# Two-tile recurrence units: where the contraction steps of the tiles stand among the seven levels

## The reference

```
def token_mixers(n, s0_fw, s0_bw, ...):
    p = n @ w_in
    v = to_heads(p[..., COL_V:COL_FFW])
    logf_fw, k_fw = hgrn2_forget(p[..., COL_FFW:COL_FBW], lb[0])
    logf_bw, k_bw = hgrn2_forget(p[..., COL_FBW:COL_Q], lb[1])
    q = to_heads(silu(p[..., COL_Q:COL_G]))
    o, s_fw, s_bw = hgrn2_bidir(q, v, logf_fw, k_fw, logf_bw, k_bw, s0_fw, s0_bw)
    ...
    u3 = short_conv(p[..., COL_HY:COL_MERGE], conv_w, conv_b)
    o_b = hyena(u3, kern, hy_bias)

def hgrn2_chunk_scan step:
    cum = cumsum(gb); decay = exp(cum[t] - cum[s]) for s <= t
    scores = einsum('bhtsd,bhsd->bhts', q[t] * decay, k)
    o = scores @ vb + (qb * exp(cum)) @ s
    s_new = exp(last) * s + einsum('bhsd,bhse->bhde', kb * exp(last - cum), vb)
```

## Time and profile before

| | |
|---|---|
| time, median of 3 runs | 3942.68 us (3938.78 to 3953.53) |
| time of the profiled execution | 3941.52 us |
| its span in the profile | 3939.7 us |
| mean granted clock of TensorE | 0.947 of full |
| PE busy | 3543.2 us, 90% of the span |
| DVE busy | 2002.5 us, 51% |
| ACT busy | 1182.0 us, 30% |
| POOL busy | 958.7 us, 24% |
| chain that ended last | PE 72%, DVE 17%, issue 6%, ACT 3% |

### The profile page before, as it was taken

How to read it: one execution, slowest core, us unless ns; L and a number is a source line. 1 busy time by engine, 2 the same in 40 slices (tenths; PEclk the granted TensorE clock), 3 DMA queues, 4 the chain that set the end, 5 groups by cost and what they waited for, 6 DMA issues and landing times.

```text
span 3939.7 us, 51314 instructions
## 1 busy us (share of the span) xinstructions
PE 3543.2 (90%) x18712; PEld 2882.8 (73%) x18712; DVE 2002.5 (51%) x3071; ACT 1182.0 (30%) x1638; POOL 958.7 (24%) x396
## 2 busy tenths in 40 slices
PE   6699999888788998999698888899999887898998
PEld 2278888777676767778577756788888666677887
DVE  5656441536654446883538666454341457662113
ACT  1132112334441123222333255321212343543222
POOL 1023222221121123444210100222223211113443
PEclk9799999998899999999899899899999988899999
DMA  4323331310122223553210010233331210112222
GB/s 179 101 96 128 124 126 70 128 59 27 33 86 67 62 91 128 182 181 125 100 40 26 33 43 22 73 119 128 117 112 64 72 43 28 54 34 79 96 96 91
DMA packets 101862, 341.43 MB, mean 87 GB/s; under 512 B 10159, under 2 KB 21551, under 8 KB 100240
## 3 DMA queue, kind: packets, MB, share of 16 engines
q1 hardware_dynamic: 82760, 301.90, 22.0%
q10 hardware_dynamic: 18952, 37.51, 2.7%
HBM read 325.21 MB, written 14.16 MB: 86 GB/s over the span
## 4 chain that ended last, share of the span: by engine, by line
PE 72%; DVE 17%; issue 6%; ACT 3%; DMA 1%; DVEq 0%; POOL 0%; ACTq 0%; POOLq 0%
PE ps L399 56%; PE ps L415 2%; PE ps L1478 2%; PE ps L1944 1%; PE ps L1489 1%; PE ps L871 1%; DVE u_Z L993 1%; DVE hid_lo L756 1%; DVE xx_lo L645 1%; DMA hyena_k<-fst 1%; DVE u_S L1031 1%; DVE u_P L1005 1%; PE ps L1930 1%; PE ps L1916 1%; PE ps L545 1%
## 5 line engine op out<-in xcount | busy, mean ns | idle before, releaser
L2203 POOL TENSOR_TENSOR wr_lo<-raw,wr_hi 128x1024 fp32r<-128x1024 f32 x392 | 958.5, 2446 | 2951.4 <-ACT wr_hi L455 2931.5
L399 PE MATMUL ps<-xx_hi,wr_hi 128*128 128x512 f32 x1840 | 742.2, 403 | 55.2 <-DVE xc_lo L649 44.0
L399 PE MATMUL ps<-xx_hi,wr_lo 128*128 128x512 f32 x1840 | 729.9, 397 | 0.0
L399 PE MATMUL ps<-xx_lo,wr_hi 128*128 128x512 f32 x1840 | 728.4, 396 | 0.0
L455 ACT ACTIVATE wr_hi<-raw 128x1024 fp32r<-128x1024 f32 x388 | 411.6, 1061 | 602.0 <-PE ps L399 569.3
L399 PEld LDWEIGHTS ps<-xx_hi,wr_hi 128*128 128x128 f32 x1840 | 349.7, 190 | 154.2 <-issue 36.2
L750 DVE TENSOR_TENSOR ff_raw<-ps,ff_gate 128x768 f32<-128x768 f32 (+1 forms) x88 | 72.6, 825 | 681.7 <-PE ps L399 678.7
L399 PEld LDWEIGHTS ps<-xx_lo,wr_hi 128*128 128x128 f32 x1840 | 350.1, 190 | 77.5 <-issue 2.2
L399 PEld LDWEIGHTS ps<-xx_hi,wr_lo 128*128 128x128 f32 x1840 | 349.6, 190 | 76.8
L500 DVE CUSTOM_DVE_ANT_0 ps<-raw,cb 128x1024 f32<-128x1024 f32 x240 | 379.9, 1583 | 50.5 <-DMA raw<-in_mod_stream 18.7
L399 PE MATMUL ps<-hid_hi,wr_hi 128*128 128x512 f32 (+1 forms) x1056 | 319.1, 356 | 9.3 <-DVE hid_lo L756 9.3
(11 more groups left out here) (338 smaller groups left out, 5383.1 us busy)
## 6 DMA issues: line engine op xcount, KB each, us to landing
raw<-in_stream SPq DMA_DIRECT2D x392, 512.0 KB, 3.3
raw<-in_mod_stream SPq DMA_DIRECT2D x168, 512.0 KB, 4.4
hK<-hyena_k ACTq DMA_DIRECT2D x4, 1152.0 KB, 6.1
h_kept<-H ACTq DMA_DIRECT2D x2, 2048.0 KB, 9.9
hyena_k<-fst ACTq DMA_DIRECT2D x14, 256.0 KB, 11.9
H<-in_h ACTq DMA_DIRECT2D x1, 3072.0 KB, 9.7
h_kept<-H ACTq DMA_DIRECT2D x1, 3072.0 KB, 8.7
H<-h_kept ACTq DMA_DIRECT2D x1, 3072.0 KB, 9.8
```

The costliest lines, as they stand in the source:

```text
L399: last = pe.matmul(gslot(slot)[:, col:col + n], w, rhs[part], start=(bi == 0 and pi == 0), stop=(bi == len(blocks) - 1 and pi == 2))
L2203: nc.gpsimd.tensor_tensor(wr_lo[:, s, :], raw[:, s % RAW, :], wr_hi[:, s, :], ALU.subtract).then_inc(tile_lo, 1)
```

## The change

The deal of the steps over the levels gets a table of its own for two tiles: the sixteen steps stand as 1, 2, 1, 2, 2, 1, 7. For one or three tiles it is as before. The first tile now ends behind level 4. In HGRN units 0 to 5 ACT reads the `hyp` tile at level 6 and not at 4, ahead of the head; in units 6 and 7 it stays at 4. ACT's places in the GLA units are as before. The diff:

```diff
@@ -422,7 +422,8 @@
         def pe_between(pe, tally, kinds, li):
 
             steps = KC * len(kinds)
-            for step in range(steps * li // len(LEVELS), steps * (li + 1) // len(LEVELS)):
+            parts = (0, 3, 6, 9, 12, 15, 18, 30) if len(kinds) == 2 else (0, 1, 2, 3, 4, 5, 6, 7)
+            for step in range(steps * parts[li] // parts[-1], steps * parts[li + 1] // parts[-1]):
                 pe_x_step(pe, tally, step % KC, kinds[step // KC])
 
@@ -1371,9 +1372,9 @@
                 def ahead(li, nxt=u + 1, u=u, hy0=at_hy):
                     if u == 7 and li == 1:
                         hy_tile(hy0 - 1)
-                    if li == 4:
+                    if li == (4 if u >= 6 else 6):
                         hy_tile(hy0)
-                    elif li == 6 and HY_TILES[u] == 3:
+                    elif li == 6:
                         hy_tile(hy0 + 1)
```

## The result

The changed kernel takes 3955.93 us (median of 20 runs, 3939.34 to 3976.2), the kernel before beside it 3940.14 us (20 runs): ratio 1.0039, 95% interval 1.0024 to 1.0053. It is 15.8 us slower, where 2.5 us faster was forecast; the time lies inside the stated range (3927 to 3957), 1 us from its upper end. Its profiled execution took 3966.26 us with a span of 3964.5 us and a mean granted clock of 0.933, against 3941.52, 3939.7 and 0.947.

The account below looks back on a forecast made before the run. PE was taken to set most of the end, DVE and ACT a part. HGRN -15.7, first GLA layer +12.5 and second +0.7 gave -2.5 us, 3939.0 from the profiled 3941.5; forecast 3940 us, range 3927 to 3957.

Parts of the forecast that it names:

- HGRN units: HGRN units 0 to 5: second parts, from level 3 to the next scores, shrink from 138.7 to 123.0 us, saving 15.7.
- the 14.6 + 20.8 of the walk: HGRN units before a backward one: 14.64 us from scores to level 3, then 20.8 to the next scores.
- First GLA layer, units 0 to 2: First tile ends 2.6 us later, ACT waits, the scan starts about 2 us later; with half clock, +9 over three units.
- Unit 3 of each layer: Last GLA units: four more steps behind level 6; +3.5 us in the first layer, +4.3 in the second.
- Second GLA layer, units 0 to 2: Border's four more steps fit PE's 3.29 us wait; transposes and output at full clock save 1.2 us in each unit.
- The slower one: Rival: half clock at the borders of all 14 units, HGRN gain about 0, about +25 us, 3966; chance 0.07.
- HGRN gains less: Rival: full 3.5 us of half clock in every HGRN unit plus POOL's wait, -8 instead of -15.7, 3948; chance 0.20.
- GLA loses less: Rival: first GLA tile comes in time since PE was ahead, +4 instead of +13, 3932; chance 0.14.
- a wait of some 2.6 us for `hx`: Sign expected in the first GLA layer's changed profile, with a scan 2 us later in each unit.
- The sum: Whole kernel: -15.7 HGRN, +12.5 first GLA layer, +0.7 second, together -2.5 us.
- the range's terms: HGRN -19 to -8, first GLA layer +6 to +17, second -3 to +6, giving 3927 to 3957 us.

Follow-up runs that it names:

- e11: e1 plus eleven unused matmuls behind level 2 and the tile's split moved behind the head, HGRN units: 3927.85 us, 0.9968 of the kernel before.
- e10: e1 with the tile's split moved behind the head in HGRN units 0 to 5: 3926.77 us, 0.996 of the kernel before.
- e2: Kernel before with the new deal of steps in the GLA units alone: 3971.04 us, 1.0081 of the kernel before.
- e7: e2 with repeated, overwritten matmuls ahead of level 1 in GLA units 1 to 3: 3959.32 us, 1.0031 of the kernel before.
- e6: e2 with ACT's read of the first tile at level 6 instead of 5: 3953.28 us, 1.0028 of the kernel before.
- e15: Kernel before with GLA steps dealt 1, 2, 1, 3, 3, 3, 3 (thin front, three at the border): 3973.85 us, 1.0104 of the kernel before.
- e5: Kernel before with GLA steps dealt 2, 2, 2, 2, 0, 1, 7, first tile ending behind level 3: 3958.76 us, 1.0045 of the kernel before.
- e13: Kernel before with the new deal in the last GLA unit of each layer alone: 3949.6 us, 1.0037 of the kernel before.
- e14: Kernel before with the new deal in GLA units 0 to 2 of each layer alone: 3966.59 us, 1.0082 of the kernel before.
- e1: Kernel before with the new deal and the moved `hyp` read in the HGRN units alone: 3926.5 us, 0.996 of the kernel before.
- e3: Kernel before with only the `hyp` read moved from level 4 to 6 in HGRN units 0 to 5: 3929.06 us, 0.9967 of the kernel before.
- e8: Kernel before, even deal, with repeated, overwritten matmuls ahead of level 1 in GLA units 1 to 3: 3945.82 us, 0.9994 of the kernel before.

## Why the prediction was wrong, point by point

**HGRN units: right.** Saved -15.7 forecast, -16.2 measured. The steps held one by one. Counted from level 3 in unit 1: level 5's exponential at 4.83 forecast, 4.81 measured; the scan at 8.4 and 8.48; the end of the last put at 18.1 and 17.79; the next scores at 20.2 and 20.13. The backward heads gave 35.4, the 14.6 + 20.8 of the walk. POOL's subtraction held DVE's 942 by 2.0 us, where 2.35 was taken. The rule named from the Trainium skill's page SBUF — State Buffer, section Who interferes with whom, is borne out for an instruction with two inputs: 2.97 under POOL, 0.96 in e11 without. The row on which the prediction rested it, 1402 with 2.75, is a TENSOR_SCALAR with one tensor as input (`lb` beside it is one value a partition), and so not of the form that the prediction names; it shows that such a form was held as well. POOL's subtraction stands in the trace from 931.56, while DVE's scan ran, and DVE's 942 only from 932.33; POOL took 2.92 there and 2.35 in e10, so it seems to have waited for the scan first and then held 942; no run tested that order by itself.

**First GLA layer, units 0 to 2: the step that failed.** The prediction put it so: "The tile's last step now has one more level and one more step of others ahead of it: 1.49 + 1.11 = 2.6." Both prices are right at full clock, and the order is right. But the sum let PE reach that place at the clock of before. It moved steps out of the levels ahead and did not ask what became of the clock there. The measured delay of the exponential of level 6 is 5.6 to 7.8 us a unit, where the walk gave 1.9 to 2.2, and the term is +24.6 instead of +9. With the clock back sooner, as in e2's units 1 and 2, the delay is 2.5 and 2.7, just what the step said; in unit 0 it is 4.9 even there, and e2's term is +15.2. Full clock in the levels (e7) brings units 1 and 2 from e2's 51.6 and 51.3 to 48.5 and 47.4, so it is the clock; the later read (e6) brings them to 49.6 and 49.5, so it acts through ACT's read, though by the units alone this is no larger than what such a unit varies by; the medians of e6 and e2 (+12.1 and +31.8) carry it. e15 and e5 show that the front makes it in units 1 and 2 and not the border.

**Unit 3 of each layer: right in the sum, by luck in part.** +3.5 forecast and +2.8 measured, +4.3 and +4.8; e13 has 4.2 and 5.0. The first is no sharper than the 2.6 by which this unit varies. Its two terms were both too small: from level 6 to the output it is 5.9 more and not 4.5, since the seven steps took 1.30 each and not 1.11, and level 6 comes 3.0 earlier, where 2.0 at most was allowed.

**Second GLA layer, units 0 to 2: wrong in unit 0.** -1.2 in each was forecast, from transposes and an output at full clock; they do run at full clock, but units 1 and 2 save 0.2 and 0.1. Unit 0 lost 6.4. PE stood at half clock from its scores to 3228.5, 26 of its 45 us; before, it was 5 us. e7, with the same deal and no fill in this unit, has the same 26 us and the same 45.0. In e2 and e14, with the same deal again, unit 0 is 40.5 and 40.4. The even deal has such long half clock in some executions too: 23 us of it in e1, whose unit is 40.2. So the loss comes where the new deal meets a long stretch of half clock, and it isn't there in every execution; no run was made for this unit, and its cause stays open.

**The rivals.** The slower one (0.07, 3966) was 10 us above the time, with the wrong place: it put half clock at the borders and the loss into HGRN too. HGRN lost nothing to it, because DVE leads there; at the GLA borders the window is 0.72, and the seven steps take 9.14 instead of the 7.8 at full clock. "HGRN gains less" (0.20, 3948) is as near to the time, 8 us below, and wrong too: HGRN gained what was forecast. "GLA loses less" (0.14) was the opposite of what came. What had been looked for as a sign, a wait of some 2.6 us for `hx`, was 6 to 8, and 3.3 to 4.8 in e2.

**The sum.** By the units -16.2 + 24.6 + 2.8 + 6.1 + 4.8 = +22.1; the medians say +15.8 (9 to 21). Of the range's terms that for HGRN was sound. The upper ones for the GLA layers were not, +17 where +27.4 came and +6 where +10.9 came: half clock was taken as a cost of the seven steps alone. That the time still lies within 3927 to 3957 is luck, since the HGRN gain stands against a GLA loss outside its own range.

What stays open: why the clock falls a second time, with no idle time of PE in the stretch, and what decides for how long. It is not the deal alone. In unit 1 the front of before has such a stretch too (3.5 us before, 3.6 in e5, none in e3), and the new deal has 9.5 us in the changed kernel and in e14, 3.6 in e2 and none in e6. What the profiles do show is that the long second stretches stand in kernels with a thin front alone, that the filled ones are free of it in that unit (e7, e8), and that each thin front leaves the half clock of unit 0 about 7 us longer.

## What to carry to other kernels

Steps taken out from between narrow matmuls can have a second price, the clock of what stays there: before thinning a stretch, read the granted clock of the levels that surround it, and walk the consumers of its last step at the low clock as well as at the high one. A result that is read in program order ahead of a critical instruction should be produced early or read late; here moving the read gave most of the gain, and moving the producer without the read cost 41 us. Where one table serves several kinds of units, try it on each kind alone: one part gained 12.7 us, and the other lost 31.8.

## What the hardware showed that was not expected

The clock was half in a stretch where the records have PE busy for 9.50 of 9.50 us (2105.5 to 2115), and for 24 us of e15 at 21.02 busy. Both hold 64-column matmuls of the levels with few steps between. The kernel before has a shorter one, 3.50 of 3.50 us (2102.2 to 2105.7), which holds steps of a projection alone, right behind a level, so narrow matmuls in the stretch are not needed for it. The Trainium skill's page TensorE: Matmul & The Clock Gate, section What's actually happening, has the clock follow "how busy the PE has been recently"; by the busy time that the profile shows, that stretch should have been at full clock, and it wasn't.

Repeating matmuls whose result is overwritten kept the clock full from level 1 to level 5 in unit 1 (e7, e8) and in unit 2 of e7; in unit 2 of e8 it fell for some 3 us all the same. It cost nothing that could be measured in e8, and bought something only where PE's last step was waited for.
